# The text's expert layer: a dense sweep over all experts replaced by a chain at the front and fetches of the chosen rows

## The reference, cut to what matters

```python
def block(hb):                       # 128 tokens
    q = (hb @ w_q).reshape(PEER_BLOCK, PEER_HEADS, 2, PEER_DHALF)
    s = jnp.einsum("nhkd,hkmd->nhkm", q, sub_keys)
    s_half, i_half = lax.top_k(s, PEER_TOPK)          # 16 of 128, twice per head
    cand = s_half[:, :, 0, :, None] + s_half[:, :, 1, None, :]
    top_s, top_c = lax.top_k(cand.reshape(...), PEER_TOPK)
    ids = k1 * PEER_KEYS + k2                         # of 16384 experts
    g = jax.nn.softmax(top_s, axis=-1)
    ue = jnp.take(u_tab, ids, axis=0)
    ve = jnp.take(v_tab, ids, axis=0)
    act = jax.nn.gelu(jnp.einsum("nd,nhkd->nhk", hb, ue))
    return jnp.einsum("nhk,nhkd->nd", g * act, ve)
```

## Time and profile before

| | us |
|---|---|
| median of 3 runs | 3841.38 |
| lowest and highest run | 3839.69, 3841.99 |
| span of the profiled execution | 3840.6 |
| TensorE busy in the span | 3733.3 |
| VectorE busy | 2959.4 |
| ScalarE busy | 1608.9 |
| GpSimd busy | 132.9 |

### The profile page before, as it was taken

One profiled execution on the slowest core, in us unless ns is written; L12 is line 12 of the kernel. 1 busy time (PEld: TensorE's weight loads), 2 busy tenths in 40 slices (PEclk: granted clock), 3 DMA queues, 4 the chain that ended last, 5 costly groups with the idle time before them and its releaser, 6 DMA issues.

```text
span 3840.6 us, 61937 instructions
## 1 busy us (share of the span) xinstructions
PE 3733.3 (97%) x21638; PEld 3165.1 (82%) x21638; DVE 2959.4 (77%) x5352; ACT 1608.9 (42%) x2440; POOL 132.9 (3%) x161
## 2 busy tenths in 40 slices
PE   8999999999999999999999999999989999999998
PEld 8896799546988888888888888888769888888887
DVE  7533175896898799999887899999475997777776
ACT  5301052232228444444494444444333284444443
POOL 0000000000000000000000000000400100000000
PEclk9999999999999999999999999999999999999999
DMA  5314454475522666665525777777745316555554
GB/s 197 105 45 147 154 195 152 156 238 180 177 89 77 202 197 190 194 196 191 188 65 192 234 240 238 237 238 233 180 150 187 126 61 197 191 191 189 192 188 153
DMA packets 203268, 667.45 MB, mean 174 GB/s; under 512 B 35888, under 2 KB 46176, under 8 KB 201456
## 3 DMA queue, kind: packets, MB, share of 16 engines
q1 hardware_dynamic: 158784, 573.12, 46.4%
q0 software_dynamic: 20016, 82.95, 7.0%
q10 hardware_dynamic: 24320, 9.37, 0.9%
HBM read 637.11 MB, written 27.21 MB: 173 GB/s over the span
## 4 chain that ended last, share of the span: by engine, by line
PE 86%; DVE 11%; DMA 2%; ACT 1%; issue 1%; DVEq 0%; SPq 0%; ACTq 0%; POOLq 0%
PE psum L1132 27%; PE psum L1118 17%; PE psum L1120 9%; PE psum L752 5%; PE psum L1230 5%; PE psum L777 4%; PE psum L692 4%; PE psum L1097 2%; PE psum L1426 2%; PE psum L1200 2%; DVE arena L2502 1%; DVE arena L2503 1%; PE psum L1177 1%; DVE arena L2504 1%; PE psum L1528 1%
## 5 line engine op out<-in xcount | busy, mean ns | idle before, releaser
L1132 PE MATMUL psum<-v_split,coef_split 128*128 128x512 f32 x4284 | 1034.0, 390 | 0.0
L1118 PE MATMUL psum<-input_split,u_split 128*128 128x512 f32 x2800 | 987.0, 391 | 0.0
L1132 PEld LDWEIGHTS psum<-v_split,coef_split 128*128 128x128 f32 x4284 | 779.7, 188 | 157.1 <-issue 1.0
L1120 PE MATMUL psum<-input_split,u_split 128*128 128x256 f32 x2800 | 788.9, 282 | 0.0
L1118 PEld LDWEIGHTS psum<-input_split,u_split 128*128 128x128 f32 x2800 | 525.3, 188 | 112.7 <-DVE u_split L2649 0.2
L1120 PEld LDWEIGHTS psum<-input_split,u_split 128*128 128x128 f32 x2800 | 528.5, 189 | 16.2
L1836 ACT ACTIVATE work<-work 128x256 f32<-128x256 f32 x350 | 146.6, 419 | 846.1 <-DVE work L2654 846.1
L1619 ACT ACTIVATE v_split<-ring 128x1024 fp32r<-128x1024 f32 x357 | 379.7, 1064 | 239.7 <-PE psum L1132 227.3
L2649 DVE TENSOR_TENSOR u_split<-ring,u_split 128x1024 fp32r<-128x1024 f32 x377 | 459.6, 1219 | 12.4 <-ACT u_split L1619 12.4
L2654 DVE TENSOR_REDUCE work<-psum 128x256 f32<-128x512 f32 x350 | 242.0, 691 | 258.9 <-PE psum L1120 257.6
L2649 DVE TENSOR_TENSOR v_split<-ring,v_split 128x1024 fp32r<-128x1024 f32 x357 | 433.9, 1215 | 2.3 <-ACT v_split L1619 2.3
(11 more groups left out here) (484 smaller groups left out, 4748.6 us busy)
## 6 DMA issues: line engine op xcount, KB each, us to landing
ring<-in_u SPq DMA_DIRECT2D x384, 512.0 KB, 3.6
ring<-in_v SPq DMA_DIRECT2D x384, 512.0 KB, 3.5
ring<-in_w SPq DMA_DIRECT2D x316, 512.0 KB, 3.6
arena<-in_ada POOLq DMA_DIRECT2D x48, 512.0 KB, 4.4
scratch_inj<-stage ACTq DMA_DIRECT2D x16, 512.0 KB, 5.3
arena<-scratch_inj POOLq DMA_DIRECT2D x7, 1024.0 KB, 7.4
scratch_cm<-work POOLq DMA_DIRECT2D x8, 512.0 KB, 5.6
scratch_cm<-arena POOLq DMA_DIRECT2D x8, 512.0 KB, 5.1
```

What stands on the lines that cost most here:

```text
L1118: mm(bank(b), rows[:, 0, P * k:P * k + P], HR[:, k, :, :], start=(k == 0), stop=False, skip_group_check=True)
L1120: last = mm(bank(b)[:, 0:S], rows[:, 1, P * k:P * k + P], HR[:, k, 0, :], start=False, stop=(k == 7), skip_group_check=True)
L1132: last = mm(bank(2 + 2 * i + f), CFR[:, b, c, P * i:P * i + P], parts[:, v, 512 * f:512 * f + 512], start=(first and c == 0 and v == 0), s ...
```

## The change

The text's whole path through layer 0 moves to the front of the kernel, before the first block. Its modulation rows, mixer, mixer output, queries and key scores are made by `text_chain` on each engine with plain float32 products. 104 weight slots (`t_rows`, `t_cm`, `t_out`, `t_q`) stand ahead of the stream for it. The mixer becomes a function that runs for 256 tokens, first for the text and later for the image; beside the image's run the modulation rows are now layer 1's. The text's gates, its dense sweep, `late_choice`, `row_product` and their stores and reloads go.

The text's experts are fetched instead. GpSimd issues 256 indirect DMAs for `u` and 256 for `v`, each bringing one chosen row of 4 KB to each of 128 partitions (one token of a half of the text on each). For `u`, VectorE multiplies each fetched block with the text's rows and accumulates along the row: one `dot`. There are two buffers for them. The dots are placed through the first block by the table `DOTS`; those it doesn't place stand in one row before the image's mixer.

```diff
+NPICK = NH * TOPK
+NFETCH = 2 * NPICK
+UBUFS, VBUFS = 2, 4
+FIRST_PICK, LAST_PICK = 27, NEXP - 3
+DOTS = {"in": 24, "misc": 7, "inverse": 3, "levels": 12, "recurrence": 23, "attention": 22, "merge": 8,
+        "add": 14, "up": 44, "down": 10}
+DOTS["rest"] = NFETCH - sum(DOTS.values())
...
+            def fetch_u(upto):
+                nonlocal fetched
+                while fetched < min(upto, NFETCH):
+                    n = fetched
+                    b = n % UBUFS
+                    if n >= UBUFS:
+                        pool.wait_ge(sem("rows_used"), n - UBUFS + 1)
+                    pool.indirect_dma_start(UROWS[b], None, u_rows, bass.IndirectOffsetOnAxis(ROW_IDS[:, n:n + 1], 0))\
+                        .then_inc(sem(f"row_fetched{b}"), 16)
+                    fetched += 1
...
+            def dot():
+                n = made["dots"]
+                made["dots"] = n + 1
+                dve.wait_ge(sem(f"row_fetched{n % UBUFS}"), 16 * (n // UBUFS + 1))
+                u = UROWS[n % UBUFS].rearrange("p (k t) -> p k t", k=4)
+                stt(u, u, 1.0, HTOK[n // NPICK], ALU.mult, ALU.mult, accum_out=WEIGHTS[:, n:n + 1])\
+                    .then_inc(sem("rows_used"), 1)
```

Within the first block, one dot follows each input tile and each up tile, two follow each residual tile, and clusters of one to eight stand before waits of the inverse, the recurrence and the attention:

```diff
                 taps_rest("conv", 4, QKV, t, 0)
+                dots("in", 1)
...
             L.take("product_ready")
             L.give(cp(OG[:, :, P:S], PS(3072, 8, P)), "gdn_out")
+            dots("recurrence", 8)
             L.take("rowsum")
...
+            dots("attention", 7)
             L.take("attention_out")
...
-            prepare_readout(0)
             prepare_lags(1)
+            dots("rest")
+            assert made["dots"] == NFETCH, made
+            dve.wait_ge(sem("rows_used"), NFETCH)
+            prepare_readout(0)
```

The `v` rows are fetched and weighed within the image's sweep from block 27 to 125, with four buffers. VectorE multiplies each by its weight and adds it to `ACCT`: one `pick`. In that sweep the subtraction for the `v` slot moves from VectorE to GpSimd, in one queue with the fetches:

```diff
+            for j in range(AHEAD[0] + 2, NEXP):
+                b = j % 2
+                pool.wait_ge(sem("v_high"), j + 1)
+                parts = USP[:, 0] if j == NEXP - 1 else VSP[:, b]
+                w = FIRST_ROW[0] + (2 * j + 2 if j < NEXP - 1 else 2 * NEXP - 1)
+                pool.tensor_tensor(parts[:, 1, :], ring[:, w % RING, :], parts[:, 0, :].bitcast(F32), ALU.subtract)\
+                    .then_inc(sem("v_low"), 1)
...
+                while j >= FIRST_PICK - 1 and picked < min(NFETCH, picks_until(j) + VBUFS):
+                    m = picked
+                    if m < VBUFS:
+                        pool.wait_ge(sem("coef_ready"), 14 + 4 * m)
+                    else:
+                        pool.wait_ge(sem("rows_used"), NFETCH + m - VBUFS + 1)
+                    c = NPICK * (m % 2) + m // 2
+                    pool.indirect_dma_start(VROWS[m % VBUFS], None, v_rows,
+                                            bass.IndirectOffsetOnAxis(ROW_IDS2[:, c:c + 1], 0))\
+                        .then_inc(sem(f"row_fetched{m % VBUFS}"), 16)
+                    picked += 1
...
                     for j in range(e + 2, NEXP - 2):
                         total(j, j % 2)
-                        low(1, j, j % 2, w0 + 2 * j + 2)
                         coef(j, j % 2)
                         low(0, j + 2, j % 2, w0 + 2 * j + 3)
...
+                        while made["picks"] < picks_until(j):
+                            pick()
```

More of the change, by code:

```diff
@@ L46 @@
 LOWEST = -3.0e38
[L47 to L50, removed]
+PARKED = (64, 80)
+AHEAD = (10, 14)
+STEADY = [sum(NEXP - n for n in AHEAD[:p]) for p in range(3)]
+NPICK = NH * TOPK
[5 more added lines that the diff above has]
+DOTS["rest"] = NFETCH - sum(DOTS.values())
 TWO_PI = 6.283185307179586
@@ L736, in keep_busy, with row_part, turn_row @@
                     mm(bank(b), ones, small[:, 0:512], start=True, stop=True)
+            def row_part(b, w, k, f):
+                q = 2 * (k % 2) + f
+                return mm(bank(b)[32 * q:32 * q + 32, :], CSP[:, k, :],
+                          ring[:, w % RING, 512 * f:512 * f + 512],
+                          start=(k < 2), stop=(k >= 6))
+            def turn_row(off, row):
+                to = PS(off, 2, 4, 2).rearrange("p f u c -> p u f c")
+                for u in range(4):
+                    last = mm(to[:, u], row[:, P * u:P * u + P], PART, start=True, stop=True, skip_group_check=True)
+                return last
@@ new lines, in first_rows @@
+            def first_rows():
+                for q in range(2):
+                    for k in range(8):
+                        arrived(L.slots)
+                        for f in range(2):
+                            last = row_part(6 + q, L.slots, k, f)
+                            if f == 0:
+                                last.then_inc(sem("slot_begun"), 1)
+                            else:
+                                L.slots += 1
+                                if k == 7:
+                                    L.mark(last, "row_ready")
+                            yield
@@ new lines, in mixer_rows @@
+            def mixer_rows(t, l0, w0, row):
+                if t % 4 == 0 and t:
+                    L.take("row_copied")
+                    if t < 16:
+                        pe.wait_ge(sem("lin_free"), l0 + t + 1)
+                    L.mark(turn_row(row_at(1 + t // 4), row), "row_turned")
+                if t == 16:
+                    return
+                for i in range(2):
+                    w, k = w0 + 3 * t + 1 + i, (2 * t + i) % 8
+                    arrived(w)
+                    for f in range(2):
+                        last = row_part(7, w, k, f)
+                        if f == 0:
+                            last.then_inc(sem("slot_begun"), 1)
+                    if k == 7:
+                        L.mark(last, "row_ready")
@@ L1163, in turn_sums @@
                         last = pe.transpose(PS(1024 + S * d + P * i, P), ACC[:, i, P * d:P * d + P], ident)
+                    if d % 4 == 3:
+                        L.mark(last, "sums_turned")
+                if not text:
+                    return
+                pe.wait_ge(sem("rows_used"), 2 * NFETCH)
+                for d in range(8):
+                    if d == 4:
+                        L.take("acc_evacuated")
+                    for i in range(2):
+                        last = pe.transpose(PS((S * d if d < 4 else 1024 + S * (d - 4)) + P * i, P),
+                                            ACCT[:, i, P * d:P * d + P], ident)
                     if d % 4 == 3:
@@ L1260, in peer_image @@
                 keep_busy(4, 7)
-                for _ in range(2):
-                    L.take("late_taken")
                 for _ in range(2):
@@ L1466, in behind @@
                     sum_part(SQC, t - 1, b=5)
-            linear(1, 8, MIXED, 512, between=behind, part=lambda k: L.take("gated"))
+            linear(1, 8, MIXED, S, between=behind, part=lambda k: L.take("gated"))
             c, l0 = UP_PARTS, L.lin - 1
@@ L2275, in _ @@
                 misc(t)
+                dots("misc", 1)
             L.take("rows_spread")
@@ L2370, in _ @@
                 sc, SH = PS(1024, 4, 512), SC[:, h, :]
+                dots("attention", 5 if half == 0 else 2)
                 L.take("scores_ready")
@@ L2383, in _ @@
                 SH = SC[:, h, :]
+                dots("attention", 4)
                 L.take("probs_exp")
```

1115 lines of the change are left out of this document (581 added, 534 removed).

## The result

| | before | after |
|---|---|---|
| median, us | 3841.08 (4 runs) | 4210.23 (4 runs) |
| lowest and highest, us | 3839.69, 3841.99 | 4205.89, 4212.77 |
| profiled span, us | 3840.6 | 4204.1 |

The change made the kernel slower: ratio 1.0963, 95% interval 1.0948 to 1.0979. The prediction had the direction but not the size; 4210 is 30 us above its range.

A forecast was written before the change was run, and what follows sets the result against it. TensorE was taken to bound the steady sweeps, VectorE the mixer with its preparation. 3841 - 815 + 350 + 258 + 125 + 247 + 12 = 4018 us; own range 3940 to 4080, 8-of-10 range 3830 to 4180.

The forecast's parts named there:

- What goes: Text's gates and dense sweep, its key scores in the image's choice, and half the mixer's tokens disappear: -815 us.
- The text chain: Text's layer 0 path in front of the first block, from modulation to choice, sharing nothing with that block: +350 us.
- A dot in a row, 2.9 us: Where dots stand in a row, two buffers and a 4.4 us landing make 2.9 us a dot.
- The leftover row: 89 unplaced dots in one row before the mixer's preparation, hidden by no work: +258 us, bounds 116 and 294.
- The dots in the first block: 167 dots placed among the first block's tiles and waits add 125 us, bounds 60 and 190.
- Small ones 6: Remaining small places for dots in the first block, the recursion's levels among them: 6 us together.
- The image sweep, 8.0 us a step: Experts with picks and GpSimd's subtraction take 8.0 us instead of 5.51, over 99 experts: +247 us.
- rival A: In the image sweep GpSimd's subtraction and VectorE's product run in turns: 8.7 us an expert, 4087 us; chance 0.28.
- it starts about 0.9 us into each expert and ends at 3.3: GpSimd's 2.36 us subtraction in the image sweep, queued behind the last fetch of the expert before.
- Rival B: In the image sweep GpSimd and VectorE work side by side: step 6.7 us, 3889 us; chance 0.17 with the slower fetch.
- C: Dense text sweep was dearer: fetches land in 2.9 us, GpSimd's subtraction is hidden, 3777 us; chance 0.13.
- D: Fetches don't keep pace in the image sweep: 2.1 us a pick, 5.5 an expert, hidden anyway; within the 0.05 for elsewhere.

The follow-up runs named there:

- Experiment 4: Changed kernel with six buffers instead of two for the fetched u rows of the 89 leftover dots: 4081.03 us, ratio 1.0634.
- Experiment 3: Changed kernel with each recursion level's two fetches issued before GpSimd's memset of that level instead of behind it: 4157.59 us, ratio 1.0827.
- experiment 8: Fastest version: four edits, picks from block 14, reloads issued without waits, 3756.26 us; then 45 recurrence and attention dots moved into the leftover row, 3768.84 us.
- experiment 2: Changed kernel without the 256 fetches of v rows; GpSimd's subtraction and VectorE's picks stay: 4075.91 us, ratio 1.0614.
- experiment 1: Changed kernel with the v slot's subtraction in the image sweep moved back from GpSimd to VectorE: 3999.92 us, ratio 1.0406.
- experiment 5: Changed kernel with the v subtraction back on VectorE and a plain float32 u product in the image sweep: 3969.82 us, ratio 1.0324.
- four local edits: Changed kernel with v subtraction on VectorE, plain u product, level fetches ahead of the memsets and six leftover-dot buffers: 3781.03 us, ratio 0.9848.
- six into 2.3%: The four-edit kernel plus picks from block 14 and the two reloads at block 120 issued without waiting: 3756.26 us, ratio 0.9768.

## Why the prediction was wrong, point by point

- **What goes** (-815) held: text sweep and added sums -782.6 against -779; mixer and choice lie within the 234.5 against 234.
- **The text chain** (+350) measured 345.3; only the sum was compared, not its seven terms.
- **A dot in a row, 2.9 us** held: 5.8 us a pair with landings of 4.1 to 4.4, the value taken from the plain loads of the earlier trace rows; the estimate of 3.2 us by the Trainium skill (DMA: Bandwidth & Descriptors, Anatomy of one DMA) is too short here. The leftover row, +258, held with it. Experiment 4 shows the cause was the two buffers.
- **The dots in the first block** (+125) measured 191. Input, residual and up tiles, 90 predicted, came to 83. The step that failed is "Small ones 6", in which the levels' dots were lumped: they cost 55 us. The sum compares the clusters with VectorE's idle time and has no term for a fetch that starts late; I had not followed what stands in GpSimd's queue ahead of the fetch. Experiment 3 shows this alone was the cause. In recurrence and attention the clusters cost 51 against 29, and experiment 8 shows that all of it is theirs. Why each costs more than I took is not shown. The chain there has landings of 5 to 8 us against my 4.4, and from 815 to 895 the granted clock is 0.79:

```profile
823.95 8.01 DMA work<-in_u_rows,H
815.00:895.00 80.00, 43.20 (x224) 30.18 (x222) 31.84 (x52) 5.47 (x5) 16.37 (x14) 0.79 0.64 213
```

The landings lie beside the ring's refills, but no run took that traffic away, so that is argued.
- **The image sweep, 8.0 us a step**, is the large miss: 9.19, or +375.9 against +247. The mechanism was rival A, given 0.28, and even its 8.7 was short. The step that failed is "it starts about 0.9 us into each expert and ends at 3.3". I let one fetch stand between VectorE's last pick and GpSimd's subtraction; there are two or three, one of them 1.75 us long, so the subtraction started 2.4 us in (2504.93 to 2507.36) and ended at 4.8. Then none of it falls into VectorE's wait for the gelu, and VectorE loses 2.7 us to it where rival A had 2.0. That is more than the 0.5 us between 8.7 and 9.2, the rest of the step being 6.5 instead of 6.7; experiment 2 shows the fetches' part of the price. The larger mistake was to settle between "side by side" and "in turns" at 8.0. Every one of the 74 experts in the window has such a wait, and experiment 1 shows that taking turns was the cause.
- **The rule cited for A** (the Trainium skill, SBUF — State Buffer, Who interferes with whom): the traces agree. VectorE's instructions with two SBUF inputs wait for GpSimd (0.43 becomes 3.16), its sum from PSUM does not: 0.69 us at 2064.68 with GpSimd's subtraction running from 2063.04 to 2065.45. The picks and dots beside GpSimd's issues are not stretched; there it is the issue that waits (experiment 4).
- **Rival B** (3889) fell with the same rows; **C** needed a landing under 4.0 us and had 4.2; **D** as forecast: the sweep's picks waited for fetches only a little, until the edits of experiment 5 made the step short.

What stays open: the attention's landings and its lower clock, and the few us by which the stages ahead of the sweep differ between executions.

## What to carry to other kernels

Moving work with SBUF inputs from VectorE to GpSimd is safe only where it falls into VectorE's idle time: the same edit cost nothing in the blocks without picks (and won nothing, TensorE being the bound) and 2 us each in those with them. A fetch must be issued from a point of its queue that doesn't itself wait for the work which the fetched data holds up; follow the queue, not only the load. And a loss that repeats per item (a landing with two buffers, a split on the bound engine) can be larger than the whole verdict: four local edits turned 9.6% slower into 1.5% faster, six into 2.3%.

## What the runs showed of the hardware

- GpSimd's issue of an indexed fetch of 128 rows takes 0.94 us with VectorE idle. Where a dot of VectorE is running as it begins, it takes 0.94 us and the rest of that dot less 0.13: the 59 such issues of experiment 4's window fit this to 0.01 us, the longest took 1.98. The 75 dots that begin during an issue keep their 1.23 us. So the issue waits for a running dot and doesn't hold up the next.
- VectorE's copy with rounding, one SBUF input, is shut out by GpSimd's subtraction as well: 0.29 us becomes 3.03 (at 2146.03, beside GpSimd's subtraction from 2146.49 to 2148.90). Of the 74 stretched instructions between 2120 and 2800, 63 are the subtraction of 256 columns, 10 this copy and one the subtraction of 1024 columns.
- 73 of these 74 begin by their records 0.45 to 0.58 us before GpSimd's subtraction, within the issue ahead of it, and wait all the same. Who starts first by the records doesn't tell who waits.
- Indexed fetches of 4 KB rows, 128 at a time, come at 367 GB/s with six buffers, 6% under the 391 GB/s of the densest plain traffic in the earlier trace rows; alone, one lands 4.2 us after its issue begins.
- After 8 us of idle TensorE, the next 32 matmuls of a level ran at 1.2 GHz, 7.06 us instead of 3.57, and with the idle time gone (experiment 3) a granted clock of 1.00 holds from 562.4 on, which is 2.4 GHz. Less than 8 us does it as well: the product at 552.2 of experiment 3 follows 2.57 us of idle time and ran at 1.2 GHz too.
